# A two-layer decoder trunk: the head norm's inverse root moved to GpSimd, output additions moved earlier in the attention steps, first and last steps rebuilt

## The chip, the core and the metric

The kernel runs on one core of a Trainium2 chip. The time is device microseconds (us) of one execution. Five engines work beside each other: TensorE (in profiles PE, its weight loads PEld), VectorE (DVE), ScalarE (ACT), GpSimd (POOL) and SyncE (SP, which here only issues DMAs). Each engine takes its instructions strictly in order and waits on semaphores.

## What is computed

A trunk of two layers on x of 1024 tokens by 1024 features, float32. Layer 0: retention, then a squared-ReLU MLP. Layer 1: sliding-window attention, then an MLP. The change touches only the attention and its borders:

```
def sliding_window_attention(h, positions, w_in, q_gain, k_gain, sinks, w_out):
    q, k, v = split(h @ w_in)            # 16 query heads, 4 key/value heads of 64
    q = rope(rmsnorm(q, q_gain)); k = rope(rmsnorm(k, k_gain))     # per head and token
    scores = q k^T * 64**-0.5            # 128 queries against the current and the previous 128 keys
    probs = softmax([masked scores, sink])[..., :-1]
    return (probs @ v) @ w_out           # added to x
```

The head norm needs 1/sqrt(mean of squares + 1e-6) for 5 heads (4 query heads, 1 key head) of each token: a tile of 128x5 numbers a step.

## The kernel before

Every product is made of three TensorE products on split numbers: a number is its rounded `hi` part (ScalarE copies it to fp32r) and the rest `lo` (VectorE subtracts). L480 to L482 are the three matmuls of the helper `product`.

The attention runs over 4 groups `g` (one key/value head and its 4 query heads) of 8 steps `s` (128 tokens each), 32 steps in all. Group 0 and group 3 are written out, groups 1 and 2 are a hardware loop. A step is a software pipeline over several token blocks. The list gives the order in which each engine works in step `s`; (t), (t-1), (t-2) is the block.

- TensorE, `sw_steps("pe")`: `a_pe` projects block t (24 matmuls); `b_pe` transposes rotated q and k of t-1; `d_pe` transposes the probabilities of t-2; half of `f_pe`, the output product with w_out (one 128x512 tile, 6 matmuls) for a block six steps back; `c_pe` scores of t-1 (6 matmuls); the other half of `f_pe`; `e_pe` probabilities times v for t-2 (12 matmuls). In step 0 of a group (a "turn") the first half of `f_pe` stands ahead of `a_pe`, because `a_pe` waits there for the weights of the new group.
- ScalarE: `sq_act` squares q, k of t (L1895); `qkT_act` hi parts of the transposes (L1920, L1921); `copy_act` (L1902, L1905); `pT_act` hi parts of the probabilities; in steps 4, 6 and 7 weight splits; `exp_act` exponentials of t-1 (L1936, L1938); `oT_act` (L1946); `prob_act` scales half of the probabilities (L1912).
- VectorE: `qkT_dve` lo parts (L1953, L1954); `vlo_dve`; `var_dve` sum of squares and variance (L2015, L2017); then `rsqrt` (L463 to L473, nine dependent instructions on 128x5) with the list `meanwhile` strewn between them, one entry after each: two `pT_dve` (L1960), two `mask_half` (L1973), two `max_dve` (L1982), then `sink_dve` (L1989 to L1993), on which the exponentials wait. Then `scale_dve` (L2025, L2031); two output additions `add` (L659), which free the banks that `f_pe` writes; `oT_dve` (L2073); `den_dve` (L1999, L2001); `prob_dve` (L2067). In step 7 the four weight splits of the next group (`sw_split_lo`, L1806) are in the list too.
- GpSimd, `rope_sw_pool`: q, k times the gain (L2043), then, after `scale_dve`, the rotation (L2051 to L2061), on which `b_pe` of the next step waits.

Banks: `f_pe` alternates between banks 7 and 1 (`BDS`), and bank 1 is also `SB`, into which `b_pe` and `qkT` work; so `b_pe` waits for the addition that read it. The down product of the layer-0 MLP ends with 16 tiles: `FILLED` = 13 of them ahead of the attention, 3 as filler in steps 0 and 1. Behind the last step, `drain_*` ends the pipeline and starts the MLP of layer 1.

Of the kernel before, what the change touches and what calls it, by code (L numbers as in the profile page):

```python
# [29 lines left out]
P = 128  # L30
# [75 lines left out]
RSQ = 9  # L106
# [21 lines left out]
def trunk(nc, x_in, positions, norm_mix, norm_mlp, w_up, w_down, ret_in, ret_out, sw_in, q_gain,  # L128
          k_gain, sinks, sw_out, c_ident, c_causal, c_mask, c_head, c_freq, c_freq_row, out, y_dram, x_dram, a_dram, r_dram):
    ctx = ExitStack()  # L130
    with ctx:
# [124 lines left out]
        with place(146) as z:  # L256
# [11 lines left out]
            htmp = sb("htmp", [P, SW_NH], F32, z)  # L268
            smax = sb("smax", [P, 4], F32, z)
# [181 lines left out]
        def rsqrt(dve, count, base, a, r, t, meanwhile=()):  # L451


            todo = list(meanwhile)
            each = -(-len(todo) // (RSQ - 1)) if todo else 0

            def step(k, ins):
                ins.then_inc(count, 1)
                for work in todo[each * k:each * (k + 1)]:
                    work()  # L460
                dve.wait_ge(count, base + k + 1)

            step(0, dve.tensor_scalar(r.bitcast(I32), a.bitcast(I32), 1, None, ALU.logical_shift_right))  # L463
            step(1, dve.tensor_scalar(r.bitcast(I32), r.bitcast(I32), -1.0, float(0x5F3759DF), ALU.mult, ALU.add))
            step(2, dve.scalar_tensor_tensor(t, r, -0.5, r, ALU.mult, ALU.mult))
            step(3, dve.tensor_tensor(t, t, a, ALU.mult))
            step(4, dve.scalar_tensor_tensor(r, t, 1.5, r, ALU.add, ALU.mult))

            c = math.sqrt(3 / 8)
            step(5, dve.scalar_tensor_tensor(t, r, c, r, ALU.mult, ALU.mult))  # L470
            step(6, dve.tensor_tensor(t, t, a, ALU.mult))
            step(7, dve.scalar_tensor_tensor(t, t, -10 / 8 / c, t, ALU.add, ALU.mult))
            step(8, dve.scalar_tensor_tensor(r, t, 15 / 8, r, ALU.add, ALU.mult))  # L473
# [188 lines left out]
        FILLED = TILES - 3  # L662
# [326 lines left out]
        def plain_dve(dve, layer, begin):  # L989
# [7 lines left out]
            if layer == 1:  # L997
                p_lo_dve(dve, layer, 7)
                norm_rstd(dve, 3, 0)
            for kk in range(4):  # L1000
                t_dve(dve, layer, 6, kk)
            between = ([lambda kk=kk: b_lo_dve(dve, layer, 6, kk) for kk in range(4)] +
# [29 lines left out]
        def plain_act(act, layer, begin, final):  # L1032
# [5 lines left out]
            for kk in range(4):  # L1038
                b_hi_act(act, layer, 5, kk, final)
            if layer == 1:  # L1040
                p_hi_act(act, layer, 7)
            for kk in range(4):
                b_hi_act(act, layer, 6, kk, final)
            if layer == 0:
                p_hi_act(act, layer, 7)
# [765 lines left out]
        def a_pe(pe, g, t):  # L1811
# [5 lines left out]
            if isinstance(g, int) and g == 0 and t % 4 == 0:  # L1817
                hT_ready(pe, t // 4)
            wait(pe, sw_vlo, i)
            product(pe, ps[:, SA, 0:SW_COLS],  # L1820
                    [(hT_hi[:, k, t * P:(t + 1) * P], hT_lo[:, k, t * P:(t + 1) * P], ws_hi[:, k, :], ws_lo[:, k, :])
                     for k in range(KT)]).then_inc(a_mm, 1)

        def b_pe(pe, g, t):
            i = TT * g + t
            pe.wait_ge(sw_radd, i + 1)
            wait(pe, sw_qlo, 2 * i)
            if not isinstance(i, int) or i > 5:
                pe.wait_ge(x_add, TILES * DG_SW + 2 * (i - 5))
# [181 lines left out]
        def var_dve(dve, g, t):  # L2011
# [4 lines left out]
            dve.wait_ge(sw_var, 2 * i + 1)  # L2016
            dve.tensor_scalar(hvar[:], hss[:], 1.0 / SW_DH, EPS, ALU.mult, ALU.add).then_inc(sw_var, 1)  # L2017

        def scale_dve(dve, g, t, meanwhile):
# [15 lines left out]
        def rope_sw_pool(pool, g, t):  # L2035
# [7 lines left out]
            pool.tensor_tensor(qk_raw[:], qk_raw[:], qkgain[:], ALU.mult).then_inc(sw_gain, 1)  # L2043
            pool.wait_ge(sw_norm, i + 1)
# [43 lines left out]
        def first_steps_pe(pe, s):  # L2088

            if s == 0:  # L2090
                norm_stat_pe(pe, 2, 0)
                a_pe(pe, 0, 0)
            if s == 1:
                a_pe(pe, 0, 1)
                fill_pe(pe, FILLED)
# [3 lines left out]
                fill_pe(pe, FILLED + 2)  # L2099
# [30 lines left out]
        def drain_act(act, s):  # L2130
            if s == TT:
                qkT_act(act, LAST, TT - 1)
                pT_act(act, LAST, TT - 2)
                for kk in (2, 3):
# [22 lines left out]
        def drain_dve(dve, s):  # L2157
            if s == TT:
# [9 lines left out]
                for t in (2, 3):  # L2168
                    edge_low(dve, 1, t)
                p_lo_dve(dve, 1, 0)  # L2170
                for m in (4, 5):
                    add(dve, DG_SW + LAST, m, BDS)
# [22 lines left out]
        def sw_steps(which, eng):  # L2195
# [28 lines left out]
            def step(g, s, last_group):  # L2224
                begins = isinstance(g, int) and g == 0
                turn = s == 0 and not begins
                if which == "pe":
# [13 lines left out]
                    run(lambda *a: f_pe(*a, 1), g, s, FLAG)  # L2241
                    run(e_pe, g, s, 2)
                if which == "act":
# [3 lines left out]
                    if begins and s == 1:  # L2247
                        last_norm_act(eng, FILLED)
# [17 lines left out]
                    if begins and s == 1:  # L2266
                        for m in (FILLED + 1, FILLED + 2):
                            last_norm_act(eng, m)
                    if last_group and s == TT - 1:
                        eng.wait_ge(a_mm, TT * SW_KV)  # L2270
                        for kk in range(2):
                            b_hi_act(eng, 1, 1, kk, SW_FINAL)
                if which == "dve":
                    if begins and s == 1:
                        fill_dve(eng, FILLED)
# [5 lines left out]
                    masks = softmax(g, s)  # L2281
# [8 lines left out]
                    if begins and s == 1:  # L2290
                        fill_dve(eng, FILLED + 2)
# [6 lines left out]
                    if begins and s < 3:  # L2298
                        for m in ((8, 9, 10), (11, 12), (13, 14, 15))[s]:
# [343 lines left out]
```

## Time and profile before

| | |
|---|---|
| median of 3 runs | 2653.89 us (2653.49 to 2654.97) |
| profiled execution | 2654.76 us |
| its span, first to last instruction | 2653.1 us |
| busy share of the span | PE 97%, PEld 81%, DVE 67%, ACT 35%, POOL 10% |
| attention, first `a_pe` to the last `qkT_dve` | 1540.5 to 1945.7 us |
| granted TensorE clock, mean | 0.99 of 2.4 GHz |

A timeline row says: start in us from the span's start, duration in us, engine, line, operation, output <- inputs, shape, count, and in brackets the idle time of the engine before it with the instruction that ended it. Starts one behind the other can lie closer than a duration, since an engine overlaps the end of one instruction with the start of the next. A row of windows gives, for a stretch, its length and the busy time of each engine (with counts), the granted clock, the DMA share and GB/s.

### The profile page before, as it was taken

Reading aid. Unit: us, or ns where it says so; the run is one execution under the profiler, and the core shown is the slowest. Engines: PE = TensorE matmul, PEld = TensorE weight load, DVE = VectorE, ACT = ScalarE, POOL = GpSimd, SP = SyncE. Lnnn points to the kernel's source line nnn. Section 1 sums busy time; section 2 is a strip of 40 time slices with the busy share of each in tenths; the row PEclk is TensorE's granted clock in tenths of the full one; section 3 lists DMA queues with packets and bytes.
Section 4 is the critical chain, followed back from the end, with each engine's and each line's share of the span. In section 5 each row is a group of like instructions: output and inputs, shape, how many; then the busy total and the mean of one; then the engine's idle time right before and its main releaser. Section 6 shows DMA issues by size and latency. Waiting matters only on the chain.

```text
span 2653.1 us, 36828 instructions
## 1 busy us (share of the span) xinstructions
PE 2569.6 (97%) x11929; PEld 2145.0 (81%) x11929; DVE 1771.6 (67%) x3397; ACT 927.8 (35%) x1732; POOL 278.2 (10%) x344
## 2 busy tenths in 40 slices
PE   8999999999999999999999978988999999999999
PEld 6888878888788888888888867877877888888887
DVE  6545454454577876667766777888878666667765
ACT  5332332323311544442111255545554444311112
POOL 2102011020000300000000052322330000000000
PEclk9999999999999999999999999999999999999999
DMA  6012120121433333353233201001023323532332
GB/s 202 31 51 69 48 74 14 48 72 48 143 96 99 123 116 123 103 177 124 95 96 101 82 21 41 17 24 40 17 76 115 127 96 110 206 96 95 95 97 85
DMA packets 161729, 231.67 MB, mean 87 GB/s; under 512 B 21681, under 2 KB 103889, under 8 KB 161618
## 3 DMA queue, kind: packets, MB, share of 16 engines
q1 hardware_dynamic: 159314, 226.10, 26.5%
q10 hardware_dynamic: 2304, 4.20, 0.4%
q8 instruction: 57, 0.93, 0.1%
q14 instruction: 54, 0.44, 0.1%
HBM read 171.53 MB, written 58.73 MB: 87 GB/s over the span
## 4 chain that ended last, share of the span: by engine, by line
PE 80%; DVE 10%; issue 5%; ACT 4%; DMA 1%; POOL 0%; SPq 0%; DVEq 0%; ACTq 0%; POOLq 0%
PE ps L480 26%; PE ps L482 26%; PE ps L481 26%; ACT xn L1936 2%; DVE smax L1982 1%; DVE hss L2015 1%; DVE pT_lo L1960 1%; PE ps L1362 0%; PE ps L1313 0%; PE ps L1345 0%; DVE xT L659 0%; PE ps L1315 0%; PE ps L1314 0%; DVE ws_lo L1806 0%; DVE hT_lo L531 0%
## 5 line engine op out<-in xcount | busy, mean ns | idle before, releaser
L659 DVE TENSOR_TENSOR xT<-ps,xT 128x512 f32<-128x512 f32 x704 | 482.2, 689 | 264.1 <-PE ps L482 263.9
L480 PE MATMUL ps<-aT_hi,wd_hi 128*128 128x512 f32 x1408 | 554.0, 393 | 23.6 <-DVE xT L659 19.6
L482 PE MATMUL ps<-aT_hi,wd_lo 128*128 128x512 f32 x1408 | 550.3, 391 | 0.0
L481 PE MATMUL ps<-aT_lo,wd_hi 128*128 128x512 f32 x1408 | 550.0, 391 | 0.0
L480 PE MATMUL ps<-bh,uw_hi 128*128 128x512 f32 x880 | 343.7, 391 | 6.8 <-DVE xn L857 6.0
L481 PE MATMUL ps<-bl,uw_hi 128*128 128x512 f32 x880 | 343.3, 390 | 0.0
L482 PE MATMUL ps<-bh,uw_lo 128*128 128x512 f32 x880 | 343.1, 390 | 0.0
L480 PEld LDWEIGHTS ps<-aT_hi,wd_hi 128*128 128x128 f32 x1408 | 265.5, 189 | 78.7 <-DVE xT L659 14.4
L482 PEld LDWEIGHTS ps<-aT_hi,wd_lo 128*128 128x128 f32 x1408 | 265.4, 189 | 55.9
L481 PEld LDWEIGHTS ps<-aT_lo,wd_hi 128*128 128x128 f32 x1408 | 265.8, 189 | 53.7
L442 ACT ACTIVATE aT_hi<-raw 128x1024 fp32r<-128x1024 f32 x80 | 80.6, 1052 | 595.7 <-PE ps L482 580.7
L480 PEld LDWEIGHTS ps<-bh,uw_hi 128*128 128x128 f32 x880 | 165.8, 188 | 42.6 <-issue 8.0
L482 PEld LDWEIGHTS ps<-bh,uw_lo 128*128 128x128 f32 x880 | 165.8, 188 | 34.5
L481 PEld LDWEIGHTS ps<-bl,uw_hi 128*128 128x128 f32 x880 | 165.8, 188 | 34.1
L1595 DVE BATCH_NORM_STATS2 bn<-ps 128x6 f32<-128x512 f32 x32 | 22.4, 699 | 176.0 <-PE ps L482 176.0
L1936 ACT ACTIVATE xn<-xn,nmax 128x256 f32<-128x256 f32 x128 | 63.6, 498 | 140.3 <-DVE sdif L1993 140.3
L766 DVE TENSOR_TENSOR uw_lo<-raw,uw_hi 128x512 fp32r<-128x512 f32 x112 | 77.0, 690 | 53.2 <-ACT uw_hi L761 52.4
L766 DVE TENSOR_TENSOR uw_lo<-us,uw_hi 128x512 fp32r<-128x512 f32 x84 | 58.0, 692 | 73.5 <-ACT uw_hi L761 73.5
L480 PE MATMUL ps<-wv_hi,hT_hi 128*128 128x512 f32 x256 | 102.5, 401 | 0.0
L480 PE MATMUL ps<-wqg_hi,hT_hi 128*128 128x512 f32 x256 | 102.1, 399 | 0.0
L449 DVE TENSOR_TENSOR aT_lo<-raw,aT_hi 128x1024 fp32r<-128x1024 f32 x80 | 97.4, 1218 | 4.4 <-ACT aT_hi L442 4.4
L482 PE MATMUL ps<-wv_hi,hT_lo 128*128 128x512 f32 x256 | 100.1, 391 | 0.0
(287 smaller groups left out, 4649.0 us busy)
## 6 DMA issues: line engine op xcount, KB each, us to landing
raw<-in_w_up SPq DMA_DIRECT2D x64, 512.0 KB, 5.6
raw<-in_w_down SPq DMA_DIRECT2D x64, 512.0 KB, 3.6
raw<-a_dram SPq DMA_DIRECT2D x64, 512.0 KB, 3.3
raw<-in_ret_w_in SPq DMA_DIRECT2D x48, 512.0 KB, 5.0
a_dram<-upost SPq DMA_DIRECT2D x64, 256.0 KB, 2.1
a_dram<-xn SPq DMA_DIRECT2D x64, 256.0 KB, 2.0
xT<-x_dram SPq DMA_DIRECT2D x24, 512.0 KB, 6.0
y_dram<-xn SPq DMA_DIRECT2D x32, 256.0 KB, 2.3
```

The source lines that it names most:

```text
L442: act.activation(dst, src, ACT.Copy).then_inc(w_hi, 1)
L449: dve.tensor_tensor(dst, src, hi.bitcast(F32), ALU.subtract).then_inc(w_lo, 1)
L480: pe.matmul(bank, ah, bh, start=(begin and i == 0), stop=False, skip_group_check=not begin)
L481: pe.matmul(bank, ah, bl, start=False, stop=False, skip_group_check=not begin)
L482: last = pe.matmul(bank, al, bh, start=False, stop=(i == len(pairs) - 1), skip_group_check=not begin)
L659: dve.tensor_tensor(xT[:, k, cols], ps[:, banks[m % len(banks)], :], xT[:, k, cols], ALU.add).then_inc(x_add, 1)
L766: dve.tensor_tensor(uw(uw_lo, s % URING), weight(i, q), uw(uw_hi, s % URING).bitcast(F32), ALU.subtract).then_inc(u_lo, 1)
L1595: dve.bn_stats(bn[:], ps[:, BO, :]).then_inc(stats, 1)
L1936: act.activation(prob[:, hh, :, :], prob[:, hh, :, :], ACT.Exp, bias=nmax[:, hh:hh + 1], accum_out=ssum[:, hh:hh + 1]).then_inc(sw_exp, 1)
L1960: dve.tensor_tensor(pT_lo[:, s, :, :], ps[:, SP_ + s, :].rearrange("p (j n) -> p j n", n=P), pT_hi[:, s, :, :].bitcast(F32), ALU.subtract) ...
L1982: dve.tensor_reduce(smax[:, 2 * j:2 * j + 2], prob[:, 2 * j:2 * j + 2, :, :].rearrange("p h s n -> p h (s n)"), axis=AX.X, op=ALU.max).the ...
L2015: dve.tensor_reduce(hss[:], qkn, axis=AX.X, op=ALU.add).then_inc(sw_var, 1)
```

## The change

1. The inverse root of the head norm moves. VectorE computes only a seed (one instruction instead of the first two; the shift is folded into a multiplication by -0.5 on the integer view). The remaining ten instructions (`rsqrt_rest`, all `tensor_tensor` on 128x5, each waiting for the one before through `sw_rsq`) run on GpSimd between the gain product and the rotation. `scale_dve` waits for them.
2. The order on VectorE: ahead of `scale_dve` stand the two `pT_dve` and the two `mask_half`; behind it the maxima and `sink_dve`, and then the output additions. In step 7 the list is: `pT_dve` x2, one output addition, masks x2, one weight split, the other output addition, three weight splits; all ahead of `scale_dve`.
3. In a turn both halves of `f_pe` stand ahead of `a_pe`, VectorE adds their results first of all, and `b_pe` of block 7 waits for these additions too (`ahead`).
4. First steps: `FILLED` is 14, fillers are 2; the first `a_pe` waits for the lo parts one feature tile at a time; normalisation work of the second half is spread otherwise over VectorE, ScalarE and GpSimd; `norm_rstd` of the second half takes the `work` list of step 3 in between.
5. Last steps: hi and lo parts for the MLP leave step 7 and go into the drain, where VectorE does the output additions 4 and 5 first, and four `edge_low` after them (two before).

```
-RSQ = 9
+RSQ = 8
+REST = 10
...
+        def rsqrt_rest(pool, count, base, a, r, t):
+            def step(k, ins):
+                ins.then_inc(count, 1)
+                pool.wait_ge(count, base + k + 1)
+            step(0, pool.tensor_tensor(t, r, r, ALU.mult))
+            step(1, pool.tensor_tensor(t, t, a, ALU.mult))
+            step(2, pool.tensor_tensor(t, hconst[:, 0, :], t, ALU.subtract))
+            step(3, pool.tensor_tensor(r, t, r, ALU.mult))
+            step(4, pool.tensor_tensor(t, r, r, ALU.mult))
...
+            step(9, pool.tensor_tensor(r, t, r, ALU.mult))
...
-        FILLED = TILES - 3
+        FILLED = TILES - 2
...
+            ahead = 2 if t == TT - 1 and not (isinstance(g, int) and g == SW_KV - 1) else 0
             if not isinstance(i, int) or i > 5:
-                pe.wait_ge(x_add, TILES * DG_SW + 2 * (i - 5))
+                pe.wait_ge(x_add, TILES * DG_SW + 2 * (i - 5) + ahead)
...
-            dve.tensor_scalar(hvar[:], hss[:], 1.0 / SW_DH, EPS, ALU.mult, ALU.add).then_inc(sw_var, 1)
+            dve.tensor_scalar(hvar[:], hss[:], HSCALE / SW_DH, HSCALE * EPS, ALU.mult, ALU.add).then_inc(sw_var, 1)
+            dve.wait_ge(sw_var, 3 * i + 2)
+            rsqrt_seed(dve, hvar[:], hrs[:]).then_inc(sw_var, 1)
...
-            dve.wait_ge(sw_var, 2 * i + 2)
-            rsqrt(dve, sw_rsq, RSQ * i, hvar[:], hrs[:], htmp[:], meanwhile)
+            dve.wait_ge(sw_rsq, REST * (i + 1))
...
             pool.tensor_tensor(qk_raw[:], qk_raw[:], qkgain[:], ALU.mult).then_inc(sw_gain, 1)
+            pool.wait_ge(sw_var, 3 * (i + 1))
+            rsqrt_rest(pool, sw_rsq, REST * i, hvar[:], hrs[:], htmp[:])
...
                     if turn:
                         run(lambda *a: f_pe(*a, 0), g, s, FLAG)
+                        run(lambda *a: f_pe(*a, 1), g, s, FLAG)
                     a_pe(eng, g, s)
...
+                    outs = out_adds(g, s)
+                    if turn:
+                        for w in outs:
+                            w()
+                        outs = []
                     run(qkT_dve, g, s, 1)
...
-                        work = lows(g, s) + splits[:2] + masks[:2] + splits[2:] + masks[2:]
+                        work = lows(g, s) + outs[:1] + scores[:2] + splits[:1] + outs[1:] + splits[1:]
+                        outs = []
                     else:
-                        work = lows(g, s) + masks
-                    scale_dve(eng, g, s, work)
-                    for w in out_adds(g, s):
+                        work = lows(g, s) + scores[:2]
...
+                    for w in work:
                         w()
+                    scale_dve(eng, g, s)
+                    for w in scores[2:] + outs:
+                        w()
                     run(oT_dve, g, s, 2)
```

## Rows read from the trace of the kernel before

**Rows 1.** The page, its first part: busy us, share of the span, instructions
```profile
PE 2569.6 (97%) x11929; PEld 2145.0 (81%) x11929; DVE 1771.6 (67%) x3397; ACT 927.8 (35%) x1732; POOL 278.2 (10%) x344
```

**Rows 2.** Waits of group 1: us in total, times, longest
```profile
DVE qT_lo L1953 <- ACT kT_hi L1921: 12.9, 6, 6.8
...
PEld ps L1853 <- ACT xn L1912: 1.8, 7, 0.3
```

**Rows 3.** One line's instructions, L1953: duration ns, first and last start
```profile
L1953 DVE TENSOR_TENSOR qT_lo<-ps,qT_hi x32: 417/425/426, 1556.6 to 1945.7; 128x256 fp32r<-128x256 f32 x32
```

**Rows 4.** Timeline of VectorE, one inner step of group 1
```profile
1697.70 0.42 DVE L1953 TENSOR_TENSOR qT_lo<-ps,qT_hi 128x256 fp32r<-128x256 f32 x1 [1.21 <-ACT kT_hi L1921]
...
1699.32 0.17 DVE L463 TENSOR_SCALAR hrs<-hvar 128x5 int32<-128x5 int32 x1
...
1700.07 0.69 DVE L1960 TENSOR_TENSOR pT_lo<-ps,pT_hi 128x512 fp32r<-128x512 f32 x1
1700.67 0.16 DVE L465 SCALAR_TENSOR_TENSOR htmp<-hrs 128x5 f32<-128x5 f32 x1
...
1702.75 0.68 DVE L1982 TENSOR_REDUCE smax<-xn 128x2 f32<-128x512 f32 x1
...
1703.46 0.16 DVE L1989 TENSOR_TENSOR smax<-smax,sink_b 128x4 f32<-128x4 f32 x1
...
1704.03 0.49 DVE L2025 TENSOR_TENSOR scr<-qk_raw,hrs 128x320 f32<-128x320 f32 x1
...
1704.96 1.28 DVE L659 TENSOR_TENSOR xT<-ps,xT 128x512 f32<-128x512 f32 x2
...
1709.07 0.42 DVE L1953 TENSOR_TENSOR qT_lo<-ps,qT_hi 128x256 fp32r<-128x256 f32 x1
```

**Rows 5.** Timeline of ScalarE, the same step
```profile
1703.95 0.51 ACT L1936 ACTIVATE xn<-xn,nmax 128x256 f32<-128x256 f32 x1 [3.65 <-DVE sdif L1993]
...
1707.98 0.51 ACT L1895 ACTIVATE scr<-ps,rstd 128x320 f32<-128x320 f32 x1
...
1708.66 0.38 ACT L1921 ACTIVATE kT_hi<-ps 128x256 fp32r<-128x256 f32 x1
```

**Rows 6.** Timeline of GpSimd, the same step (L2058 waits for L2053)
```profile
1705.61 0.32 POOL L2053 TENSOR_TENSOR kr<-scr,coss 128x64 f32<-128x64 f32 x1
1706.01 0.46 POOL L2058 TENSOR_TENSOR scr<-scr 128x128 f32<-128x128 f32 x1
...
1707.05 0.26 POOL L2061 TENSOR_TENSOR kr<-kr,scr 128x32 f32<-128x32 f32 x1
```

**Rows 7.** Windows: an early step with PE idle, and a turn
```profile
1584.00:1597.20 13.20, 9.27 (x54) 7.86 (x54) 10.01 (x41) 5.36 (x18) 3.37 (x7) 1.00 0.00 0
...
1643.00:1652.00 9.00, 8.97 (x42) 8.11 (x42) 2.12 (x6) 2.48 (x7) 1.48 (x5) 0.78 0.00 0
```

**Rows 8.** Timeline of the second turn, VectorE and PE
```profile
1731.82 0.42 DVE L1953 TENSOR_TENSOR qT_lo<-ps,qT_hi 128x256 fp32r<-128x256 f32 x1
...
1734.79 2.35 DVE L1806 TENSOR_TENSOR ws_lo<-raw,ws_hi 128x1024 fp32r<-128x1024 f32 x2
...
1742.86 1.28 DVE L659 TENSOR_TENSOR xT<-ps,xT 128x512 f32<-128x512 f32 x2
...
1743.60 0.80 PE L480 MATMUL ps<-aT_hi,wd_hi 128*128 128x512 f32 x1 [6.10 <-DVE xT L659]
...
1751.91 0.38 PE L1832 MATMUL ps<-ident,scr 128*128 128x128 f32 x2
...
1753.32 0.42 DVE L1953 TENSOR_TENSOR qT_lo<-ps,qT_hi 128x256 fp32r<-128x256 f32 x1 [7.59 <-ACT kT_hi L1921]
```

**Rows 9.** One line's instructions, L1989: duration ns min/median/max
```profile
L1989 DVE TENSOR_TENSOR smax<-smax,sink_b x32: 161/163/1194, 1561.6 to 1951.4; 128x4 f32<-128x4 f32 x32
```

**Rows 10.** Timeline of PE and VectorE in the first steps
```profile
1540.52 0.41 PE L480 MATMUL ps<-ws_hi,hT_hi 128*128 128x384 f32 x1 [2.94 <-DVE hT_lo L531]
...
1571.48 0.42 DVE L1953 TENSOR_TENSOR qT_lo<-ps,qT_hi 128x256 fp32r<-128x256 f32 x1 [4.41 <-ACT kT_hi L1921]
```

More of the change, by code:

```diff
@@ L470, in rsqrt @@
[L470 to L473, printed above, removed]
+            step(0, rsqrt_seed(dve, a, r))
+            step(1, dve.scalar_tensor_tensor(t, r, -0.5, r, ALU.mult, ALU.mult))
+            step(2, dve.tensor_tensor(t, t, a, ALU.mult))
+            step(3, dve.scalar_tensor_tensor(r, t, 1.5, r, ALU.add, ALU.mult))
@@ L1037, in plain_act @@
                 h12_act(act, layer, kk, final)
[L1038 to L1045, printed above, removed]
+            for i in (5, 6):
+                for kk in range(4):
+                    b_hi_act(act, layer, i, kk, final)
+            p_hi_act(act, layer, 7)
             for s in range(3):
@@ L1816, in a_pe @@
                     pe.wait_ge(x_add, TILES * DG_SW - 3)
-            if isinstance(g, int) and g == 0 and t % 4 == 0:
-                hT_ready(pe, t // 4)
+            if isinstance(g, int) and g == 0 and t == 4:
+                hT_ready(pe, 1)
             wait(pe, sw_vlo, i)
-            product(pe, ps[:, SA, 0:SW_COLS],
-                    [(hT_hi[:, k, t * P:(t + 1) * P], hT_lo[:, k, t * P:(t + 1) * P], ws_hi[:, k, :], ws_lo[:, k, :])
-                     for k in range(KT)]).then_inc(a_mm, 1)
+            pairs = [(hT_hi[:, k, t * P:(t + 1) * P], hT_lo[:, k, t * P:(t + 1) * P], ws_hi[:, k, :], ws_lo[:, k, :])
+                     for k in range(KT)]
+            if isinstance(g, int) and i == 0:
+                for k in range(KT):
+                    pe.wait_ge(n_lo, TILES + k + 1)
+                    last = product(pe, ps[:, SA, 0:SW_COLS], pairs[k:k + 1], begin=k == 0)
+                last.then_inc(a_mm, 1)
+            else:
+                product(pe, ps[:, SA, 0:SW_COLS], pairs).then_inc(a_mm, 1)
         def b_pe(pe, g, t):
@@ L2133, in drain_act @@
                 pT_act(act, LAST, TT - 2)
-                for kk in (2, 3):
+                act.wait_ge(a_mm, TT * SW_KV)
+                for kk in range(4):
                     b_hi_act(act, 1, 1, kk, SW_FINAL)
@@ L2167, in drain_dve @@
                     sink_dve(dve, LAST, TT - 1, j)
-                for t in (2, 3):
+                for m in (4, 5):
+                    add(dve, DG_SW + LAST, m, BDS)
+                for t in range(4):
                     edge_low(dve, 1, t)
                 p_lo_dve(dve, 1, 0)
-                for m in (4, 5):
-                    add(dve, DG_SW + LAST, m, BDS)
                 oT_dve(dve, LAST, TT - 2)
@@ L2240, in step @@
                     run(c_pe, g, s, 1)
-                    run(lambda *a: f_pe(*a, 1), g, s, FLAG)
+                    if not turn:
+                        run(lambda *a: f_pe(*a, 1), g, s, FLAG)
                     run(e_pe, g, s, 2)
@@ L2266, in step @@
                     if begins and s == 1:
-                        for m in (FILLED + 1, FILLED + 2):
+                        for m in (FILLED, FILLED + 1):
                             last_norm_act(eng, m)
[L2269 to L2272, printed above, removed]
                 if which == "dve":
-                    if begins and s == 1:
-                        fill_dve(eng, FILLED)
+                    outs = out_adds(g, s)
[3 more added lines that the diff above has]
+                        outs = []
                     run(qkT_dve, g, s, 1)
@@ L2298, in step @@
                     if begins and s < 3:
[L2299 removed]
+                        for m in ((8, 9, 10), (11, 12, 13), (14, 15))[s]:
                             norm_low(eng, m)
[L2301 to L2305 removed]
                 if which == "pool":
                     rope_sw_pool(eng, g, s)
[L2308 to L2309 removed]
+                    if begins and s == 1:
+                        norm_pool(eng, 2, 1, (6, 7))
             def group(g, last_group):
```

55 lines of the change are left out of this document (32 added, 23 removed).

## The prediction, written before the changed kernel was run

> **What bounds the kernel now.** I read the page first: PE is busy for 97% of the span [rows 1], so only the stretches where it is not busy can give anything back, and every stretch where it is busy can be made worse by a slower neighbour. The change works in the attention. There I read the waits of one group, then the timelines of VectorE, ScalarE and GpSimd through one inner step, then one turn and the first steps.
>
> The waits of group 1 show something that the busy share hides. PE waits for ScalarE's scaled probabilities at every step (7 times, 1.8 us in all), and VectorE waits for ScalarE's `kT_hi` at the head of its step (6 times, 12.9 us with the turn's) [rows 2]. So PE is not what sets the step, though it has only about 0.25 us to spare in each; the ring between VectorE and ScalarE is. Closing the ring by hand, with T0 the start of `qT_lo` at 1697.70:
>
> - T0 to the first exponential: 1703.95 - 1697.70 = 6.25 us, all of it VectorE's queue [rows 4, 5].
> - exponentials, denominator, scaled probabilities, to the next squares: 1707.98 - 1703.95 = 4.03 [rows 5].
> - squares and the two hi copies, to the end of `kT_hi`: 1708.66 + 0.38 - 1707.98 = 1.06, and 0.03 to VectorE [rows 4, 5].
>
> The sum is 11.37, and the next T0 is 1709.07, 11.37 later [rows 4]. Nothing is left over: each 0.1 us that VectorE puts between T0 and the exponentials makes the step 0.1 us longer. PE's own step is about 11.37 - 0.25 = 11.1 us.
>
> The 32 steps run from 1556.6 to 1945.7 by `qT_lo` [rows 3]. Of the 31 intervals 24 are plain ones of about 11.4; three are turns (20.7, 21.5 and 20.3 us, of which the second stands in the rows [rows 8]); three are the first steps; one leads into the drain.
>
> **The plain step.** *VectorE's side.* The seed starts where L463 started, T0+1.62, since it replaces that instruction; two `pT_lo` and two masks follow at 0.60 each (the spacing of 1700.07 and 1700.67) and end their issue at T0+1.70+2.40 = T0+4.10 [rows 4]. The old small instructions cost little here: about 0.07 each between large ones, so taking eight away gives back some 0.5 us, not 8 x 0.17. Behind them now stand scale and rotation, 1704.96 - 1704.03 = 0.93, ahead of the maxima. Then two maxima, 0.60 to the second and 0.71 from it to `smax` (1702.75 to 1703.46), and 0.49 from `smax` to the exponential (1703.46 to 1703.95) [rows 4, 5]. If GpSimd were never waited for, the exponential would start at 4.10 + 0.93 + 1.31 + 0.49 = T0+6.83, 0.58 later than now. That is the least the new order costs, because the exponentials now stand behind the 0.93 of `scale_dve`. The output additions moved behind `sink_dve` are no cost: they lie in ScalarE's exponentials.
>
> *GpSimd's side.* No 128x5 `tensor_tensor` ran on GpSimd. The nearest row is 128x32 at 0.26; 128x64 took 0.32 and 128x128 0.46 [rows 6], a slope of about 0.0022 us an element, so 128x5 comes to about 0.19. Waiting for its own predecessor costs 0.08 more (L2053 ends at 1705.93, L2058 starts at 1706.01 [rows 6]). Ten steps of 0.27 are 2.7 us; with the row of 0.26 unreduced, 0.34 a step, 3.4. The seed ends at T0+1.79 and GpSimd starts 0.08 later: it is done at T0+4.57 (upper bound T0+5.27), against VectorE's T0+4.10. I take 0.27, since the three sizes lie on a line. Then the exponential starts at 4.57 + 0.93 + 1.31 + 0.49 = T0+7.30: +1.05 us a step. Lower bound +0.58, upper +1.75.
>
> *A small third part.* `smax` and `sdif` now run while GpSimd rotates (it starts at about T0+5.2 and takes 2.7, so until T0+7.9, and `smax` comes at T0+6.8). The same `smax` took 0.163 us as a rule and 1.194 once, when GpSimd worked beside it [rows 9]. I add 0.15 a step (0 to 0.3): +1.20 in all. The Trainium skill says why in "SBUF — State Buffer", Who interferes with whom: a VectorE instruction with two SBUF inputs and a GpSimd instruction that reads SBUF lock each other out for a whole instruction. By that rule each of the two small instructions could wait for up to one 0.46 rotation piece, which would make the part 0.9 and not 0.15.
>
> 24 plain steps x 1.20 = **+28.8 us**. PE then idles about 1.4 us in each; an early step with 3.9 us of idle still has the clock at 1.00 [rows 7], so I charge no clock for it.
>
> **The turns.** Now PE sits idle for 6.10 us until VectorE reaches the additions at 1742.86 [rows 8], and then runs at the lower level for a while (0.78 over the next 9 us [rows 7]). The change gives PE both halves of `f_pe` early, so that this wait goes. But what is late next? Work it from T0 of step 7: seed 1.62, `pT_lo` x2 to 2.9, addition 3.5, masks 4.7, one large split (2.35 for two [rows 8]) 5.85, addition 6.45, three splits (1.15 + 0.60 + 0.60) 8.8, scale and rotation 9.7, maxima 11.0, exponential 11.5. `smax` to exponential came at 9.6 before; the exponential is 1.9 later. Then 4.0 to the probabilities, 15.5. Now VectorE's two additions of the next step come first, 16.7, and `b_pe` waits for them, because bank 1 is also its own; from `b_pe` to the next `qT_lo` it is 1753.32 - 1751.91 = 1.41 [rows 8]: T0' = 18.1. PE has finished `a_pe` by about 13.2 and idles 3.5 us, so one stall goes and a shorter one comes, perhaps with a short stay at 1.2 GHz; I take 18.2. Three turns: 54.6 in place of 62.5, **-7.9 us** (-12 if `b_pe` is not held, -3 with the clock down).
>
> **First steps.** The first `a_pe` waited 2.94 for the lo parts [rows 10]; the 14th tile (1.4 us of PE work) now covers it, and PE keeps its clock. But block 0 is a chain, not a throughput: squares, seed, ten GpSimd steps where VectorE had nine at 0.2, rotation. I get the first `qT_lo` 2.0 us earlier. The long interval until 1571.48 is ScalarE's, which waits behind the last normalisation squares [rows 10]; one such pair fewer stands there, but the exponentials come 0.5 later. **-1.6 us** (-5 to +1).
>
> **Drain.** VectorE puts the additions ahead and two more lo parts (0.60 to 0.66 each) ahead of the last denominator, so the last probabilities come about 1.2 later; the additions remove a PE wait of the same size, which lies off that path. **+1.2 us** (-2 to +3).
>
> **Sum.** 28.8 - 7.9 - 1.6 + 1.2 = +20.5. On the profiled execution's own span, 2653.1, that is 2673.6, and with the 1.66 us around it (2654.76) 2675.3; that execution lies 0.87 above the median, so the median comes to 2653.9 + 20.5 = **2674.4 us**.
>
> **Rivals.**
> - *GpSimd's step is much dearer than the line says* (0.40: a completion that costs as much again as the 0.19). GpSimd is done at T0+5.87, +2.35 a step with no contention, +56 - 8.3 = 2702. For: nothing so small ran there. Against: 0.08 measured on the same queue. Chance 0.12.
> - *GpSimd is never waited for* (0.22 a step or less). +0.58 a step: 13.9 - 8.3 = +5.6, 2659.5. It lies just at the edge of what can be told. Chance 0.12; with a turn that gives a little more it is no change.
> - *The other side, faster: the exponentials have slack after all.* If PE, not the ring, sets the plain step (its waits of 0.25 being queue latencies), the later exponentials are absorbed, the plain steps stay at 11.4 and only borders and turns count: -8.3, 2645.6. It decides from a ring no more than 0.1 us longer than now. Against: the ring closes to 0.01 us, and VectorE does wait at its head. Chance 0.16.
> - *My forecast*, slower by 12 to 37 us: 0.60. Its own range, 2666 to 2691.
>
> About 0.2% (5.3 us) is what a measurement of this kernel can tell from no change. Faster: 0.16. Within: 0.10 (most of it from the second rival). Slower: 0.74. The range for 8 in 10 leaves out the dear GpSimd step above and most of the faster case below: 2652 to 2696.
>
> **What would show it.** In the changed profile: `qT_lo` starts 12.5 us apart in the plain steps (11.4 would refute the ring); `scale_dve` waiting about 0.5 for GpSimd; the 128x5 steps on GpSimd 0.27 apart; the exponential 7.3 to 7.5 behind `qT_lo`; PE idle 1.2 to 1.5 a step ahead of `d_pe`; turns of 18 us with PE waiting ahead of `b_pe` for an addition and not ahead of `f_pe`. Wrong would make it: a GpSimd step outside 0.22 to 0.34, or turns far from 18.

## The result, and the profile after

The changed kernel took **2681.59 us** (median of 4 runs, 2678.43 to 2682.27) against 2653.99 for the kernel before: ratio 1.0101, 95% interval 1.0084 to 1.0119. It is slower by 27.6 us; 2674.4 was predicted, with 2652 to 2696 as the range and 2666 to 2691 as the likeliest case's own. The profiled execution's span is 2680.6 us, 27.5 more than before.

The page of the changed kernel, its first part; VectorE has 294 instructions fewer and GpSimd 323 more than in [rows 1]:

```profile
PE 2569.8 (96%) x11929; PEld 2148.8 (80%) x11929; DVE 1757.5 (66%) x3103; ACT 926.9 (35%) x1732; POOL 337.7 (13%) x667
```

PE does the same work in the same busy time, so the 27.5 us are time in which it waits. The waits of group 1 of the changed kernel (engine, instruction, what ended the wait; then us in total, times, longest) say before what:

```profile
PEld ps L1882 <- ACT xn L1941: 12.8, 7, 2.6
PE ps L1882 <- ACT xn L1941: 11.2, 7, 2.4
DVE aT_lo L2108 <- ACT aT_hi L1975: 10.4, 7, 2.5
...
DVE qT_lo L1982 <- ACT kT_hi L1950: 8.0, 6, 2.0
```

L1882 is `d_pe` (the transposes of the probabilities), L1941 the scaling of the probabilities. PE's weight loads waited 1.8 us for them in seven times in [rows 2]; now it is 12.8 in seven. PE itself did not wait for them before, and now waits 11.2, which is 1.6 a step.

One plain step, timeline of VectorE in the changed kernel, to be laid beside [rows 4]; T0 is `qT_lo`, now L1982:

```profile
1707.04 0.42 DVE L1982 TENSOR_TENSOR qT_lo<-ps,qT_hi 128x256 fp32r<-128x256 f32 x1 [1.21 <-ACT kT_hi L1950]
...
1708.65 0.17 DVE L479 TENSOR_SCALAR hrs<-hvar 128x5 int32<-128x5 int32 x1
1708.73 1.28 DVE L1989 TENSOR_TENSOR pT_lo<-ps,pT_hi 128x512 fp32r<-128x512 f32 x2
1709.93 1.28 DVE L2002 SCALAR_TENSOR_TENSOR xn<-ps,swmask 128x512 f32<-128x512 f32 x2
1711.61 0.49 DVE L2056 TENSOR_TENSOR scr<-qk_raw,hrs 128x320 f32<-128x320 f32 x1 [0.40 <-POOL hrs L496]
1712.14 0.49 DVE L2062 TENSOR_TENSOR scr<-scr,sins 128x320 f32<-128x320 f32 x1
1712.55 1.27 DVE L2011 TENSOR_REDUCE smax<-xn 128x2 f32<-128x512 f32 x2
1713.86 0.21 DVE L2018 TENSOR_TENSOR smax<-smax,sink_b 128x4 f32<-128x4 f32 x1
1714.10 0.39 DVE L2021 TENSOR_SCALAR nmax<-smax 128x4 f32<-128x4 f32 x1
...
1719.70 0.42 DVE L1982 TENSOR_TENSOR qT_lo<-ps,qT_hi 128x256 fp32r<-128x256 f32 x1
```

The same step on GpSimd, ScalarE and PE:

```profile
1708.90 0.20 POOL L486 TENSOR_TENSOR htmp<-hrs 128x5 f32<-128x5 f32 x1 [0.52 <-DVE hrs L479]
1709.18 0.20 POOL L487 TENSOR_TENSOR htmp<-htmp,hvar 128x5 f32<-128x5 f32 x1
...
1711.38 0.20 POOL L496 TENSOR_TENSOR hrs<-htmp,hrs 128x5 f32<-128x5 f32 x1
...
1714.59 0.51 ACT L1965 ACTIVATE xn<-xn,nmax 128x256 f32<-128x256 f32 x1 [4.95 <-DVE sdif L2022]
...
1718.76 1.09 PE L1882 MATMUL ps<-ident,xn 128*128 128x128 f32 x8 [1.43 <-ACT xn L1941]
```

The reader is to see: the interval is 12.66 instead of 11.37; `scale_dve` (L2056) waits 0.40 for the tenth GpSimd step and starts at T0+4.57, with the two maxima behind it; the exponential starts at T0+7.55 instead of T0+6.25; from there to the next T0 it is 5.11 us, against 5.12 before; and PE stands still for 1.43 us.

Where the 27.5 us lie, by the starts of `qT_lo` and of later instructions that both traces have (us, after minus before):

| stretch | predicted | measured |
|---|---|---|
| to the first `qT_lo` (1556.43, was 1556.58) | -2.0 | -0.15 |
| next three intervals (42.83, were 40.61) | +0.4 (the rest of -1.6) | +2.2 |
| 24 plain steps | +28.8 | +31.5 |
| three turns (18.82, 21.35, 18.79; were 20.72, 21.49, 20.34) | -7.9 | -3.6 |
| interval into the drain, and drain | +1.2 | +4.1 |
| start of the MLP | none | -6.5 |

### The profile page after: what moved, and what is told of

It is laid out like the page before. It is cut to its first block and busy times, and to the rows that moved or that the text cites. A ratio compares the mean times of both kernels' runs of the same rounds, so it can differ in the third digit from the quotient of the medians.

```text
span 2680.6 us, 36963 instructions
## 1 busy us (share of the span) xinstructions
PE 2569.8 (96%) x11929; PEld 2148.8 (80%) x11929; DVE 1757.5 (66%) x3103; ACT 926.9 (35%) x1732; POOL 337.7 (13%) x667
```

## The experiments

All medians in us; each ratio is against the kernel before, timed on the same chip in the same session (2654.4, 2654.4 and 2653.7 in the three sessions). The changed kernel was timed in a session of its own, so a median set against 2681.59 also carries the difference between sessions. "Kernel 2" below is the kernel of experiment 2, and "kernel 5" that of experiment 5. "Plain steps" are the 24 intervals that are neither turns nor first steps nor drain.

| kernel | experiment | median | ratio, 95% interval |
|---|---|---|---|
| e1_maxima_first | 2 | 2629.66 | 0.9908 (0.9892 to 0.9925) |
| e2_mlp_start | 6 | 2648.18 | 0.9977 (0.9967 to 0.9986) |
| e3_ring_double | 1 | 2671.8 | 1.0066 (1.0049 to 1.0083) |
| e4_unrolled | 4 | 2678.31 | 1.0093 (1.0076 to 1.0109) |
| e5_root_on_vector | 3 | 2702.0 | 1.0185 (1.0168 to 1.0202) |
| e6_drain | 8 | 2629.09 | 0.9911 (0.9894 to 0.9927) |
| e7_turn | 5 | 2622.54 | 0.9886 (0.9869 to 0.9902) |
| e8_norm_sums | 7 | 2630.86 | 0.9915 (0.9899 to 0.9932) |
| e9_old_drain | 8 | 2620.30 | 0.9871 (0.9854 to 0.9887) |
| e10_sums_between | 7 | 2620.94 | 0.9874 (0.9857 to 0.9890) |
| e11_all | 9 | 2616.71 | 0.9859 (0.9843 to 0.9875) |

**1. Does the ring really set the plain step?** The kernel before, with one maximum of 128x512 done twice on VectorE, ahead of the exponentials:

```diff
 # max_dve, j == 0
+dve.tensor_reduce(spare[:], <the same half of prob>, axis=AX.X, op=ALU.max)
 dve.tensor_reduce(smax[:, 2 * j:2 * j + 2], ...)
```

> The kernel before with one more 128x512 maximum a step on VectorE, ahead of the exponentials, its result unused (0.60 us of VectorE's queue). Ring theory: each of the 24 plain steps and of the turns becomes 0.60 longer, 16 to 18 us in all: 2670 to 2672 us, plain interval 11.97. Rival, PE sets the plain step and VectorE, busy only 9.8 of 11.4 us, has slack: 0 to 3 us, 2654 to 2657, plain interval 11.4.

Timeline of VectorE and ScalarE in one plain step of this kernel; the doubled maximum is L1986, the exponentials are L1938:

```profile
1693.62 0.43 DVE L1955 TENSOR_TENSOR qT_lo<-ps,qT_hi 128x256 fp32r<-128x256 f32 x1 [1.21 <-ACT kT_hi L1923]
...
1698.01 0.68 DVE L1986 TENSOR_REDUCE spare<-xn 128x2 f32<-128x512 f32 x1
1698.60 0.68 DVE L1988 TENSOR_REDUCE smax<-xn 128x2 f32<-128x512 f32 x1
...
1700.47 0.51 ACT L1938 ACTIVATE xn<-xn,nmax 128x256 f32<-128x256 f32 x1 [5.28 <-DVE sdif L1999]
...
1705.59 0.42 DVE L1955 TENSOR_TENSOR qT_lo<-ps,qT_hi 128x256 fp32r<-128x256 f32 x1 [1.21 <-ACT kT_hi L1923]
```

The doubled instruction takes 0.60 from start to start, the exponential starts at T0+6.85 instead of T0+6.25, and the plain interval is 11.97 against 11.37: the step grew by just what was put in. The 24 plain steps together are 14.7 us longer, and the median, 2671.8, lies in the expected interval. The ring of VectorE, busy for 67% of the span, and ScalarE sets the plain step here.

**2. The order alone.** The changed kernel, with the two maxima and the sinks put ahead of `scale_dve`, as they were before (in step 7 at the end of its list); the root stays on GpSimd:

```diff
-work = lows(g, s) + scores[:2]
+work = lows(g, s) + scores
...
-for w in scores[2:] + outs:
+for w in outs:
```

> The changed kernel with the two maxima and sink_dve put back ahead of scale_dve in every step; the inverse root stays on GpSimd. Ring theory (VectorE and ScalarE wait for each other in a ring, and what counts is the distance from qT_lo to the first exponential): that distance is 1.70 + 4 x 0.60 + 1.31 + 0.49 = 5.9 us in place of 7.55, the ring would close at 11.0, under PE's own 11.1 to 11.2, so PE sets the plain step; 24 steps x 1.5 = 36 us less than the changed kernel and 3 to 4 less at the turns: 2641 us (2634 to 2648), and smax to exponential back at 0.49, since GpSimd no longer rotates beside it. Rival, GpSimd itself is the cost (its ten steps, and its reads beside VectorE): then the order matters little and the time stays above 2670.

One plain step of this kernel, VectorE and then GpSimd:

```profile
1687.96 0.42 DVE L1982 TENSOR_TENSOR qT_lo<-ps,qT_hi 128x256 fp32r<-128x256 f32 x1 [1.22 <-ACT kT_hi L1950]
...
1692.05 1.27 DVE L2011 TENSOR_REDUCE smax<-xn 128x2 f32<-128x512 f32 x2
1693.35 0.16 DVE L2018 TENSOR_TENSOR smax<-smax,sink_b 128x4 f32<-128x4 f32 x1
1693.55 0.17 DVE L2021 TENSOR_SCALAR nmax<-smax 128x4 f32<-128x4 f32 x1
...
1693.73 0.49 DVE L2056 TENSOR_TENSOR scr<-qk_raw,hrs 128x320 f32<-128x320 f32 x1
...
1698.99 0.42 DVE L1982 TENSOR_TENSOR qT_lo<-ps,qT_hi 128x256 fp32r<-128x256 f32 x1
...
1692.33 0.20 POOL L496 TENSOR_TENSOR hrs<-htmp,hrs 128x5 f32<-128x5 f32 x1
```

The plain step is 11.02 us, 1.65 less than in the changed kernel and 0.35 less than before. GpSimd's tenth step starts at T0+4.37 and ends at T0+4.57, 1.2 us before `scale_dve` starts at T0+5.77, so its whole latency is hidden. `nmax` takes 0.17 again (0.39 above), as GpSimd's rotation, which starts at 1694.35, is no longer beside it; `smax` to exponential is 0.47 instead of 0.73. In these steps PE does not stand still at all (windows from one `qT_lo` to the next have it busy for 11.02 of 11.02 us), so 11.02 is also PE's own step as far as the trace tells; no run tried whether a still shorter ring would give more. The total lies 4 us below the expected interval. Of the 52.6 us of span between this kernel and the changed one, 24 plain steps give 39.6, the first three intervals 4.9, the turns 4.2, the interval into the drain and the drain 2.8, and this execution reached the first `qT_lo` 1.3 earlier: the ring acts in more places than in the plain steps.

**3. The place of the root alone.** The changed kernel with its new order, but the eight steps of the root on VectorE, between and behind the large instructions:

```diff
 def scale_dve(dve, g, t, meanwhile):
-    dve.wait_ge(sw_rsq, REST * (i + 1))
+    dve.wait_ge(sw_var, 2 * i + 2)
+    rsqrt(dve, sw_rsq, RSQ * i, hvar[:], hrs[:], htmp[:], meanwhile)
 # rope_sw_pool
-    rsqrt_rest(pool, sw_rsq, REST * i, hvar[:], hrs[:], htmp[:])
```

> The changed kernel with the inverse root of the head norm back on VectorE, as eight steps of its own, and everything else of the change left as it is: scale and rotation still ahead of the maxima, turns, first steps and drain as changed. My theory: the loss is the order (scale and rotation ahead of the maxima), not the place of the root. VectorE then has three small steps between the four large instructions (0.07 each) and four dependent ones of 0.20 behind them, so scale_dve starts about T0+5.1, against T0+4.97 when GpSimd had the root and was waited for: plain steps 12.7 to 12.85 us (12.67 in the changed kernel), total 2683 to 2688. The rival, that GpSimd's root (its latency of 0.28 a step and the contention) is what costs: without it the plain steps fall to 12.2 to 12.3, total about 2670.

The size was missed. The T0+4.97 of the expectation was my misreading: in the changed kernel `scale_dve` starts at 1711.61 - 1707.04 = T0+4.57. Here it starts at 1716.84 - 1711.73 = T0+5.11, 0.54 later, and the interval is 13.20, 0.53 longer. But seven of the 24 plain steps take 14.0. Timelines of VectorE and PE over a step of 13.20 and the one of 14.06 behind it:

```profile
1711.73 0.42 DVE L1982 TENSOR_TENSOR qT_lo<-ps,qT_hi 128x256 fp32r<-128x256 f32 x1 [1.21 <-ACT kT_hi L1950]
...
1716.84 0.49 DVE L2054 TENSOR_TENSOR scr<-qk_raw,hrs 128x320 f32<-128x320 f32 x1
...
1728.81 0.69 DVE L2002 SCALAR_TENSOR_TENSOR xn<-ps,swmask 128x512 f32<-128x512 f32 x1 [0.75 <-PE ps L505]
...
1723.99 1.59 PE L1882 MATMUL ps<-ident,xn 128*128 128x128 f32 x8 [1.96 <-ACT xn L1941]
```

The windows of two such steps (PE, PEld, DVE, ACT, POOL busy, granted clock, DMA share, GB/s):

```profile
1711.70:1724.90 13.20, 11.24 (x66) 10.24 (x65) 11.48 (x32) 6.95 (x22) 3.52 (x7) 0.98 0.00 1
1724.90:1739.00 14.10, 12.91 (x71) 11.60 (x70) 10.45 (x32) 5.95 (x20) 3.50 (x7) 0.90 0.28 76
```

PE waits 1.96 us at the end of the step, its clock falls for a while (mean 0.90 over the next step), the score products come late, and the masks wait 0.75 us for them. The DMA traffic in the second window is not the cause: in four of the seven long steps the DMA share is at most 0.01, and all seven have a clock of 0.88 to 0.90. Nor does the clock fall each time: three steps in a row with 1.95 to 2.15 us of idle, from 1788 to 1828, stayed at 1.00. In the changed kernel, where a plain step with 1.43 us of idle followed another, the clock stayed at 1.00.

With this kernel the plain step has been measured with both places of the root and both orders:

| plain step, us | maxima ahead of `scale_dve` | maxima behind it |
|---|---|---|
| root on VectorE | 11.37 (before) | 13.20 (this one) |
| root on GpSimd | 11.02 (kernel 2) | 12.67 (changed) |

So GpSimd's root is a gain in either order, 0.35 and 0.53 us a step (20.4 us of the median in the new order, 5.8 of it in the seven long steps); the loss in the plain steps is the order alone, 1.65 and 1.83.

**4. The loop's edge.** The changed kernel with groups 1 and 2 written out:

```diff
-with eng.Fori(1, SW_KV - 1) as g:
+for g in range(1, SW_KV - 1):
     group(g, False)
```

> The changed kernel with groups 1 and 2 written out instead of run as a hardware loop. Theory: the middle turn (21.35 us against 18.8 for the other two) is longer because VectorE's first work of the second pass, the two additions that b_pe waits for, comes 2.45 us late with no wait before it, which is the loop's jump back: written out, the middle turn is 18.8 as well and the time 2.5 us less, 2679 us. Rival: something of group 2 itself (a load, a semaphore): the middle turn stays at 21.35.

VectorE and PE at the middle turn, first in the changed kernel:

```profile
1763.12 1.29 DVE L682 TENSOR_TENSOR xT<-ps,xT 128x512 f32<-128x512 f32 x2 [2.45 <-issue]
...
1764.46 0.69 PE L1861 MATMUL ps<-ident,scr 128*128 128x128 f32 x2 [6.09 <-DVE xT L682]
```

then with the groups written out:

```profile
1759.13 1.28 DVE L682 TENSOR_TENSOR xT<-ps,xT 128x512 f32<-128x512 f32 x2
...
1760.56 0.41 PE L1861 MATMUL ps<-ident,scr 128*128 128x128 f32 x2 [3.64 <-DVE xT L682]
```

The middle turn fell from 21.35 to 18.33, and PE's wait by just 2.45. The median, 2678.31, is near the 2679 expected, but its runs (2677.56 to 2679.38) overlap those of the changed kernel, so the turn shows it and the total does not. At the loop's end VectorE waits 2.45 us for no data; the change put the two additions, for which `b_pe` waits, right behind that point.

**5. The turn's additions.** Kernel 2 (maxima first), the two additions moved from the head of step 0 to the end of step 7, where VectorE waits for the exponentials:

```diff
-if turn:
-    for w in outs: w()
+if s == TT - 1 and not last_group:        # behind scale_dve
+    for c in range(2):
+        add(eng, DG_SW + g, 2 * (TT - FLAG) + c, BDS)
 run(oT_dve, g, s, 2)
```

> The kernel with the maxima ahead of scale_dve (2629.7), and the two output additions of a turn moved from the head of VectorE's next step 0 to the end of step 7, behind scale_dve and ahead of oT_dve, where VectorE waits for the exponentials. If b_pe waits for nothing but these additions in a turn (5.1 us in the turn at the loop's edge, 2.4 in the others), the turns fall from 17.2, 20.3 and 17.2 to 15.5 to 16 each, since what is left is the splits ahead of the maxima: 7 us in all, 2622 to 2624. The rival, that the loop's edge itself costs PE or VectorE the same 3 us wherever the additions stand: the middle turn stays 2.5 to 3 longer than the others, 2625 to 2627.

The turns are 15.64, 16.81 and 15.66 us (17.25, 20.32, 17.17 in kernel 2). First instruction of VectorE behind the loop's edge:

```profile
1734.90 0.42 DVE L1982 TENSOR_TENSOR qT_lo<-ps,qT_hi 128x256 fp32r<-128x256 f32 x1 [2.36 <-issue]
```

The 2.36 us are still there, but they lie beside ScalarE's probabilities and PE's work, and make the middle turn 1.16 longer than the others instead of 3.1. The median, 2622.54, is as expected; the middle turn, expected at 15.5 to 16, is not.

**6. The start of the MLP.** The kernel before with this one edit of the change (ScalarE's order likewise):

```diff
 if layer == 1:
-    p_lo_dve(dve, layer, 7)
     norm_rstd(dve, 3, 0)
 for kk in range(4):
     t_dve(dve, layer, 6, kk)
+if layer == 1:
+    p_lo_dve(dve, layer, 7)
```

> The kernel before with one part of the change alone: at the start of the second MLP the last plain weight piece (p_lo 7, p_hi 7) stands behind the first t/b work, so that the norm's root is not held behind it. The prediction charged nothing for this part. Theory: it is what took PE's wait ahead of the MLP from 6.0 to 1.7 us and the low clock behind it away: 6.5 us less than before, 2647.5 us. Rival: the wait shrank only because the attention ended later and loads had arrived: no change, 2654.

In the kernel before, VectorE waited with the root of the last norm behind it:

```profile
2002.75 0.69 DVE L748 TENSOR_TENSOR uw_lo<-raw,uw_hi 128x512 fp32r<-128x512 f32 x1 [4.36 <-ACT uw_hi L743]
2003.36 0.16 DVE L564 TENSOR_SCALAR var<-ps 128x8 f32<-128x8 f32 x1
...
2024.39 0.77 PE L480 MATMUL ps<-bh,uw_hi 128*128 128x512 f32 x1 [6.02 <-DVE xn L857]
```

with the edit, PE at the same place:

```profile
2020.85 0.47 PE L480 MATMUL ps<-bh,uw_hi 128*128 128x512 f32 x1 [2.04 <-DVE xn L857]
```

The wait is 3.98 shorter. The rest is the clock: over the 8.6 us behind the wait it was 0.72 before, and it is 1.00 with the edit. The median fell by 6.2, to 2648.18, where 2647.5 was expected. This is the gain of 6.5 us in the changed kernel, to which I had given no price at all.

**7. The first steps.** Kernel 2, with three of GpSimd's five norm sums ahead of the attention and four behind step 1:

```diff
-norm_pool(pool, 2, 1, (1, 2, 3, 4, 5))
+norm_pool(pool, 2, 1, (1, 2, 3))
...
-norm_pool(eng, 2, 1, (6, 7))
+norm_pool(eng, 2, 1, (4, 5, 6, 7))
```

> The kernel with the maxima ahead of scale_dve (2629.7), and GpSimd has only three of the five norm sums ahead of the attention, the other two stand behind step 1's rotation with the last two. Theory: two of VectorE's small root steps took 1.20 us each because GpSimd's 128x512 sums ran beside them; without the sums they take 0.17, and the first qT_lo comes 2.0 to 2.4 earlier, at about 1552.9. The four sums behind step 1 then hold GpSimd until about 1571.8, and the gain multiplication of step 2 comes 2 to 2.5 later, so that the next intervals give most of it back: 2628 to 2631. The rival, that these steps were long for another reason: they stay at 1.20 and the first qT_lo at 1555.2.

VectorE's root of the norm ahead of the first step, in the changed kernel:

```profile
1541.56 1.20 DVE L469 TENSOR_TENSOR rtmp<-rtmp,var 128x4 f32<-128x4 f32 x1
...
1542.99 1.20 DVE L473 SCALAR_TENSOR_TENSOR rtmp<-rstd 128x4 f32<-128x4 f32 x1
```

and with fewer sums beside it:

```profile
1540.30 0.16 DVE L469 TENSOR_TENSOR rtmp<-rtmp,var 128x4 f32<-128x4 f32 x1
...
1540.69 0.16 DVE L473 SCALAR_TENSOR_TENSOR rtmp<-rstd 128x4 f32<-128x4 f32 x1
```

The first `qT_lo` came at 1552.63 instead of 1555.16, and the next interval was 15.47 instead of 13.23. The expectation put this down to the gain multiplication behind the four sums, but that one starts only at 1569.21, behind the second `qT_lo` at 1568.09. ScalarE's timeline shows the cause:

```profile
1564.79 0.63 ACT L543 ACTIVATE raw<-xT 128x512 f32<-128x512 f32 x1 [1.66 <-POOL xn L562]
...
1566.47 0.63 ACT L543 ACTIVATE raw<-xT 128x512 f32<-128x512 f32 x1 [0.43 <-POOL xn L562]
```

Its last two normalisation squares wait 2.09 us for GpSimd's sums (L562), and the head norm's squares and the hi copies, for which `qT_lo` waits, stand behind them. By the fourth `qT_lo` 0.9 of the 2.5 us is left, and the median, 2630.86, is inside the expected interval.

On the 1.20 us the Trainium skill has a rule in "SBUF — State Buffer", Who interferes with whom: a VectorE instruction with two SBUF inputs and a GpSimd instruction that reads SBUF contend for a port pair that is locked exclusively. The trace agrees: 1.20 beside a sum, 0.16 without one.

On top of kernel 5, split as three, two behind step 0 and two behind step 1:

> The same kernel at 2622.5 with GpSimd's norm sums split 3, 2 and 2: three ahead of the attention, two behind step 0's rotation, two behind step 1's. With the sums 3, 4 and 4 behind each other (three ahead, four behind step 1) the first qT_lo came 2.5 us earlier, and the next interval was 15.5 instead of 12.1, which gave it back. Theory: in step 0 GpSimd has about 2.5 us free behind the rotation, so two sums of 1.6 cost the next gain multiplication 0.5 at most, and the gain of the early root stays: first qT_lo at about 1552.4, intervals 12.5, 12.8, 12.5, total 2620 to 2621.5. The rival, that ScalarE's waits for the sums or VectorE's collisions move with them: the first three intervals together are 39 or more and the total is 2622 to 2624.

The median fell by 1.6, to 2620.94, inside the expected interval. The first `qT_lo` was expected too early (1554.00, not 1552.4: this execution reached the attention 0.9 us later). ScalarE's two waits for the sums are gone. By the fourth `qT_lo` the kernel is 0.84 ahead of kernel 5 and had begun 0.90 behind, so the split is worth 1.7.

**8. The drain.** Two attempts. First kernel 2 with two of the four lo parts behind the last probabilities:

```diff
-for t in range(4):
+for t in range(2):
     edge_low(dve, 1, t)
-p_lo_dve(dve, 1, 0)
 oT_dve(...); den_dve(...); prob_dve(...)
+for t in range(2, 4):
+    edge_low(dve, 1, t)
+p_lo_dve(dve, 1, 0)
```

> The kernel with the maxima ahead of scale_dve (2629.7), and in the drain VectorE does only two of the four edge_low ahead of the last denominator, the other two and the first p_lo behind the last probabilities. If VectorE's queue is what holds the last probabilities (exponentials done at 1933.3, denominator only at 1936.5), then PE's wait of 3.9 us ahead of the last d_pe falls to about 1.1, and a wait of about 0.7 comes ahead of p_pe: 2.0 us in all (1 to 2.5), 2627.7. The rival, that ScalarE or PE sets the drain anyway: the later waits (the MLP's start) grow by what is gained, total 2629 to 2630.

PE's waits in the drain, first in kernel 2, whose last `qT_lo` is at 1924.27:

```profile
1937.89 1.09 PE L1882 MATMUL ps<-ident,xn 128*128 128x128 f32 x8 [3.92 <-ACT xn L1941]
```

then with the edit, last `qT_lo` at 1922.33:

```profile
1934.02 1.95 PE L1882 MATMUL ps<-ident,xn 128*128 128x128 f32 x8 [1.99 <-ACT xn L1941]
...
1936.86 0.77 PE L503 MATMUL ps<-bh,uw_hi 128*128 128x512 f32 x1 [0.89 <-issue]
```

The wait shrank by 1.93 (2.8 was expected), and all of it went again: the eight transposes took 1.95 instead of 1.09, as the clock was 0.51 over the 4 us from 1934 on, where kernel 2 had 1.00 during its transposes, and PE waited 0.89 behind them. The first product of the MLP starts 14.53 us behind the last `qT_lo`, against 14.47. It needs the same lo parts: VectorE's first `p_lo` ends at 1936.75, just before that product, so moving them behind the probabilities mostly moved the wait. The median is 0.6 lower, within what scatters; this edit gives nothing.

Then kernel 5 with the last step and the drain as they were before the change:

```diff
 # step 7 of the last group, VectorE (ScalarE's hi halves likewise)
+for m in range(2): edge_low(eng, 1, m)
 # drain
+for t in (2, 3): edge_low(dve, 1, t)
+p_lo_dve(dve, 1, 0)
 for m in (4, 5): add(dve, DG_SW + LAST, m, BDS)
-for t in range(4): edge_low(dve, 1, t)
-p_lo_dve(dve, 1, 0)
```

> The kernel with the maxima ahead of scale_dve and the turn's additions at the end of step 7 (2622.5), with the last step and the drain put back as they were before the change: two of the four edge lo parts and their ScalarE halves at the end of step 7, the additions 4 and 5 behind the lo parts. The changed drain makes PE wait 3.8 us ahead of the last d_pe, and the granted clock is 0.50 for the 4 us behind it; in the kernel before there was no wait there and the clock was 1.00. Theory: the place of the two lo parts is the drain's loss. VectorE then reaches the denominator 2 to 2.8 us earlier, PE waits about 1, and the clock stays up, which saves 1 to 2 more: 3 to 4.5 us from the last qT_lo to the first product of the MLP, total 2618 to 2620. The rival, that the wait comes with PE's shorter work per step (the ring is 0.35 us shorter, PE has nothing else to do there), whatever the order: the wait stays above 3 and the total at 2621.5 to 2623.

PE no longer waits ahead of the last `d_pe` but 2.68 us ahead of an addition's tile, and the clock was 0.68 and 0.90 in the 8 us behind it. From the 31st `qT_lo` to PE's short wait in the MLP (the one of 0.52 us, which every trace has) it is 58.4 us before, 62.5 in the changed kernel, 59.7, 61.0 and 59.7 in kernels 2, 5 and the one with the sums between (all with the changed drain), and 59.3 and 58.0 in the two with the old one. So the old drain is better by some 1.5 us on the mean, half of what was expected, beside a scatter of 1.3 between kernels with the same drain: that it is better at all is likely, not shown. Neither case of the expectation was met.

**9. Together.** The old drain, the split sums and the written-out groups on kernel 5:

> Both of these together, and groups 1 and 2 written out in place of the hardware loop, which takes the rest of the edge out of the middle turn (16.8 us against 15.65 in the others). If the parts add up: 2622.5 - 3.5 - 1.8 - 1.2 = 2616 (2614 to 2618.5). If the drain and the first steps give nothing, 2621.

2616.71 us (2615.82 to 2617.54), near the 2616 expected, 37 us below the kernel before and 65 below the changed one. The turns are 15.64 three times. The page's first line:

```profile
PE 2558.2 (98%) x11929; PEld 2139.4 (82%) x11929; DVE 1743.7 (67%) x3103; ACT 927.1 (35%) x1732; POOL 340.3 (13%) x667
```

## Why the prediction was right, and where it was not

- **The ring sets the plain step: right, and shown** by the doubled maximum (+0.60 for 0.60) and by the maxima put first (1.65 us a step back). With that the rival "the exponentials have slack" falls; "GpSimd is never waited for" falls by the wait of 0.40 at each step.
- **GpSimd's step, 0.27: right.** The ten steps lie 0.275 apart (1708.90 to 1711.38), each 0.20 long; the dear step of the first rival (0.40) did not come. Taken from three larger shapes on a line, it gave T0+4.57, and `scale_dve` started at T0+4.57.
- **The contention, 0.15: too small.** `smax` to exponential is 0.73 instead of 0.49, so 0.24, most of it in `nmax` (0.39 for 0.17). The exponential came at T0+7.55 where 7.45 was predicted, and the step grew by 1.30 for 1.20: most of the 31.5 us for 28.8. The 0.9 a step that the rule of two inputs would have allowed did not come, and the rule does not name the instruction that grew: `smax` and `sdif` have two inputs (0.21 for 0.16, and 0.15 as before), `nmax` has one.
- **PE keeps its clock in the plain steps: nearly right.** 1.43 us of idle a step left it at 1.00. It fell beside the first steps and the turns, where PE idles longer, and that cost time in one plain step: the one from 1886.77, behind a step with 2.7 us of idle, had a clock of 0.91 and took 13.21. It was nearer to falling in the other steps too than I thought: with 1.96 us of idle a step (experiment 3) seven were hit.
- **The turns, -7.9: mis-sized, -3.6 measured.** That `b_pe` would be held for the additions was right, and two turns of 18.8 are near 18.2; 0.6 in each of the three makes 1.8 of the 4.3 missed. The other 2.5 is the loop's edge, which was missing: 2.45 us in which VectorE issues nothing, which I had not looked for in the trace of before, where no needed instruction stood behind it.
- **The first steps, -1.6: wrong sign, +2.1.** The nine steps at 0.2 that the prediction priced are the head norm's. It had no term for the layer norm's root ahead of them on VectorE (`rtmp`); two of its steps took 1.20, since the change has GpSimd do five norm sums there instead of two. So PE's first `a_pe` came 2.5 us earlier, but from it to the first `qT_lo` it took 18.4 us instead of 16.1. Without the collision the first `qT_lo` comes 2.5 us earlier (experiment 7), which would make about -2.7 where -2.0 was predicted. The next three intervals, 2.2 us longer in sum, carry the longer ring; kernel 2 has them at 37.96 against 42.83, so all of that loss goes with the order.
- **The drain, +1.2: too small, +4.1.** With the maxima first 2.8 us of it are gone, and with the old placement perhaps 1.5 more. The mechanism (lo parts ahead of the last denominator) fits the old placement's gain, but that gain is not clear of the scatter; I left out that the last step is a ring step too and that PE's idle takes the clock down (0.50 over 1989 to 1993).
- **The start of the MLP: not in the sum, -6.5.** The diff moved a `p_lo_dve` with a wait of 4.36 us past a root that the next layer's scales wait for. I read the moved lines only for their own cost. Without it the change would have cost 34 us. The four terms that the prediction did price came out 13.6 us too low in sum, and this one, left out, took 6.5 of them back: that the total came out 7.2 us above 2674.4 owes that much to luck.

## What to carry to other kernels

When engine A waits for B at every step and B for A, add up the ring from the timeline; if it closes, as here to 0.01 us, an instruction put between its two waits costs its full length (0.60 for 0.60), whatever the busy shares say, and one moved out of it is a gain, at most until another engine has no pause left (here PE, at 11.02). Give a latency to another engine and put what consumes it last in the queue: with the maxima ahead of `scale_dve` the ten small GpSimd steps were never waited for, with the maxima behind it they were, 0.40 us a step, and the exponentials stood behind `scale_dve` besides. Read each moved line for what it waits for as well as for what it costs, and look where a hardware loop closes before putting critical work at the head of its body.

## What the runs showed of the hardware

- A `tensor_tensor` of 128x5 on GpSimd took 0.20 us, and 0.275 from one to a dependent next; on VectorE such steps lay 0.20 apart (1716.24, 1716.44, 1716.64), so a dependent step was dearer on GpSimd by 0.075 us.
- At the hardware loop's edge VectorE issued nothing for 2.34 to 2.59 us in each of the eight kernels that have a ready instruction there (2.45 in the changed one, 2.59 and 2.36 in kernels 2 and 5). How it splits into jump, instruction fetch and anything else was not measured.
- A 128x4 instruction of VectorE with its inputs in SBUF took 1.20 us beside GpSimd's 128x512 sums, 0.16 without them; `nmax`, 128x4 with one input, took 0.39 beside GpSimd's rotation, 0.17 without it.
- PE's clock stayed at 1.00 in plain steps of 12.67 us with 1.43 us of idle that followed each other. Of eight steps of 13.2 to 13.4 with 1.95 to 2.15 us of idle (experiment 3) and a plain step behind them, five were followed by one with a mean of 0.88 to 0.90, and three by one at 1.00 or near it. What lies between was not tried.
